# Where TensorE's filler work stands in a mixture-of-experts stage: products moved between routing, early and last expert pairs

## The reference, cut to what matters

```python
combine = jnp.einsum('tk,tke->te', gate, jax.nn.one_hot(e_idx, N_EXPERTS))
for e in range(N_EXPERTS):
    h = jax.nn.silu(xt @ w_gate[e]) * (xt @ w_up[e])
    y = y + combine[:, e:e + 1] * (h @ w_down[e])
...
h = _layernorm(DEEPNORM_ALPHA * h + ffn, ln_ffn_g[layer], ln_ffn_b[layer])
```

## Time and profile before

| | us |
|---|---|
| median of 3 timed runs | 1013.69 |
| lowest and highest | 1008.77, 1015.44 |
| time of the profiled execution | 1008.44 |
| span in its trace | 1006.5 |
| TensorE busy | 959.6 (95%) |
| mean DMA rate over the span | 276 GB/s read |

### The profile page before, as it was taken

One profiled execution on the slowest core, in us unless ns is written; L12 is line 12 of the kernel. 1 busy time (PEld: TensorE's weight loads), 2 busy tenths in 40 slices (PEclk: granted clock), 3 DMA queues, 4 the chain that ended last, 5 costly groups with the idle time before them and its releaser, 6 DMA issues.

```text
span 1006.5 us, 9999 instructions
## 1 busy us (share of the span) xinstructions
PE 959.6 (95%) x3984; PEld 512.8 (51%) x3984; DVE 298.7 (30%) x773; ACT 224.0 (22%) x466; POOL 15.2 (2%) x29
## 2 busy tenths in 40 slices
PE   8989999999999999989899999999998999999986
PEld 7644875554543335333385557888445334453321
DVE  4230162331521213120234433564316112121203
ACT  1120243221211112110211533431532111111101
POOL 2000000000000000000000000000000000000001
PEclk9999999999999999999999999999999999999999
DMA  8982424152789999999994423352555899999994
GB/s 274 335 316 85 160 92 167 43 209 83 302 327 388 422 421 421 421 419 422 398 386 143 168 84 124 127 210 82 210 209 218 323 406 421 421 421 421 418 419 165
DMA packets 65779, 278.84 MB, mean 277 GB/s; under 512 B 8852, under 2 KB 9216, under 8 KB 41920
## 3 DMA queue, kind: packets, MB, share of 16 engines
q1 hardware_dynamic: 63856, 271.60, 68.5%
q0 software_dynamic: 1872, 6.53, 1.9%
HBM read 277.04 MB, written 1.06 MB: 276 GB/s over the span
## 4 chain that ended last, share of the span: by engine, by line
PE 83%; DMA 11%; DVE 4%; ACT 1%; issue 1%; SPq 0%; DVEq 0%
PE bank L679 78%; DMA ring<-in_moe_w_up 10%; PE bank L1040 2%; DMA ring<-in_w_in_ab 1%; PE bank L1097 1%; PE bank L1045 1%; PE bank L1393 1%; PE bank L775 1%; ACT feat L1461 0%; PE bank L956 0%; DVE stat L2241 0%; ACT rstd L1461 0%; DVE feat L2223 0%; DVE hT L2248 0%; DVE h L2478 0%
## 5 line engine op out<-in xcount | busy, mean ns | idle before, releaser
L679 PE MATMUL bank<-ring,hT 128*64 128x512 f32 (+1 forms) x832 | 276.7, 597 | 8.9 <-DMA ring<-in_moe_w_up 4.1
L679 PE MATMUL bank<-ring,feat 128*64 128x512 f32 (+1 forms) x1152 | 226.3, 594 | 8.6 <-ACT feat L1461 4.1
L679 PEld LDWEIGHTS bank<-ring,hT 128*64 128x64 f32 (+1 forms) x832 | 109.8, 162 | 165.8 <-issue 157.8
L679 PE MATMUL bank<-hT,ring 128*128 128x256 f32 x768 | 168.4, 380 | 1.2 <-DMA ring<-in_w_in_ab 1.0
L679 PEld LDWEIGHTS bank<-hT,ring 128*128 128x128 f32 x768 | 145.8, 191 | 21.2 <-DMA ring<-in_w_in_ab 1.7
L679 PEld LDWEIGHTS bank<-ring,feat 128*64 128x64 f32 (+1 forms) x1152 | 74.3, 131 | 150.2 <-issue 140.8
L1461 ACT ACTIVATE feat<-bank 32x512 f32<-32x512 f32 (+3 forms) x128 | 61.1, 494 | 393.3 <-PE bank L679 251.3
L679 PE MATMUL bank<-ring,yT 128*128 128x512 f32 x256 | 112.8, 595 | 0.0
L2231 DVE COPY feat<-bank 32x512 f32<-32x512 f32 (+1 forms) x56 | 38.5, 687 | 150.4 <-PE bank L679 149.8
L679 PEld LDWEIGHTS bank<-ring,yT 128*128 128x128 f32 x256 | 47.8, 190 | 55.5 <-issue 54.6
L2223 DVE TENSOR_TENSOR feat<-feat,bank 128x512 f32<-128x512 f32 x16 | 11.0, 688 | 185.7 <-PE bank L679 185.7
(11 more groups left out here) (249 smaller groups left out, 549.9 us busy)
## 6 DMA issues: line engine op xcount, KB each, us to landing
ring<-in_moe_w_up SPq DMA_DIRECT2D x64, 1024.0 KB, 16.4
ring<-in_moe_w_gate SPq DMA_DIRECT2D x56, 1024.0 KB, 14.4
ring<-in_moe_w_down SPq DMA_DIRECT2D x56, 1024.0 KB, 13.0
ring<-in_w_in_ab SPq DMA_DIRECT2D x24, 1024.0 KB, 9.1
ring<-in_w_in_cd SPq DMA_DIRECT2D x24, 1024.0 KB, 12.7
ring<-in_w_out_ab SPq DMA_DIRECT2D x8, 1024.0 KB, 5.8
ring<-in_moe_w_down SPq DMA_DIRECT2D x16, 512.0 KB, 17.9
ring<-in_w_out_cd SPq DMA_DIRECT2D x8, 1024.0 KB, 6.1
```

Source lines behind the costliest of these rows:

```text
L679: return nc.tensor.matmul(o, l, r, start=start, stop=stop)
```

## The change

- `carry` for token block 0 moves from pairs 0 and 1 into `second_lists`, around `ranks(layer, 1)`: one matmul before it and one behind. `carry` for block 1 moves to the last pair, in front of `hid_turn` and in front of the last down product. The first spreading of block 1 then starts its banks (`start=True`).
- The gate product goes to bank 1 and the turned combine weights to bank 2; the pulls' banks are changed to suit.
- Chunks 0 and 1 of the gate products of pairs 1 and 2 (`AHEAD`) are done in the filler places of the pair before: chunk 0 in front of `hid_turn`, chunk 1 behind it.
- `weights_turn` of each quad goes from behind the odd pair's up product to the place in front of it.
- The gate product of pair 4 is interleaved with the last two gather products, as pair 0's already was.

```diff
+AHEAD = (1, 2)
-        first_pulls = ((0, 1, 0, 1), (2, 3, 0, 1))
+        first_pulls = ((0, 2, 0, 2), (1, 3, 0, 2))
+        second_pulls = ((0, 1, 2, 3), (1, 0, 2, 3))
...
+            def carry(layer, t, q):
+
+                if t == 0:
+                    claim(f"ffn{layer}", 4 + q)
+                nc.tensor.matmul(bank[4 + 2 * t + q][:, :], residual, h[:, t, q * 512:(q + 1) * 512],
+                                 start=t == 0, stop=False, skip_group_check=True)
...
                 pull(layer, 0, 0, 3)
+                carry(layer, 0, 0)
                 ranks(layer, 1)
+                carry(layer, 0, 1)
                 pull(layer, 0, 1, 0)
...
+                def gate_chunks(at, ks):
+
+                    i, pair = divmod(at, 2)
+                    if ks[0] == 0:
+                        claim(f"gate{layer}_{i}{pair}", 1)
+                        held_w[at] = [weights(at, e, KC) for e in range(2)]
+                    for k in ks:
+                        for e in range(2):
+                            last = mm(bank[1][e * 2 * SLOTS:(e + 1) * 2 * SLOTS, :],
+                                      slots_of(xg[i % 2][:, k, :], pair, e), held_w[at][e](k), k == 0, k == KC - 1)
+                        if k == KC // 2 - 1:
+                            last.then_inc(half_used, 1)
+                        if k == KC - 1:
+                            last.then_inc(ready[1], 1)
+
+                def first_gate(at):
+
+                    half = 2 * at // PAIRS
                     for j in range(4):
-                        pulled(0, j)
...
+                        pulled(half, j)
+                        gate_chunks(at, (2 * j, 2 * j + 1))
                         if j < 2:
-                            pull(layer, 0, 1, j + 2)
-                    last.then_inc(ready[2], 1)
+                            pull(layer, half, 1, j + 2)
...
                     for pair in range(2):
                         at = 2 * i + pair
...
+                        if at in (0, PAIRS // 2):
+                            first_gate(at)
                         else:
...
+                            gate_chunks(at, range(2 if at in AHEAD else 0, KC))
+                        if pair:
+                            claim(f"weigh{layer}_{i}", 2)
+                            pe.wait_ge(selw_ready, QUADS * layer + i + 1)
+                            weights_turn(2).then_inc(ready[2], 1)
                         claim(f"up{layer}_{i}{pair}", 3)
...
-                        if pair:
-                            claim(f"weigh{layer}_{i}", 1)
-                            pe.wait_ge(selw_ready, QUADS * layer + i + 1)
-                            weights_turn().then_inc(ready[1], 1)
-                        elif i:
+                        if i and not pair:
                             spread_out(i - 1, 0, 0)
                             spread_out(i - 1, 1, 0)
-                        if i == 0:
-                            carry(pair, 0)
+                        if at + 1 in AHEAD:
+                            gate_chunks(at + 1, (0,))
+                        if at == PAIRS - 1:
+                            carry(layer, 1, 0)
                         claim(f"hid{layer}_{i}{pair}", 0)
                         wait_stored(pe, f"up{layer}_{i}{pair}", 3)
                         hid_turn().then_inc(ready[0], 1)
...
-                        if i == 0:
-                            carry(pair, 1)
+                        if at + 1 in AHEAD:
+                            gate_chunks(at + 1, (1,))
+                        if at == PAIRS - 1:
+                            carry(layer, 1, 1)
                         wait_stored(pe, f"hid{layer}_{i}{pair}", 0)
```

More of the change, by code:

```diff
@@ L345, in moe_jobs @@
                         for j in range(4):
-                            job(f"pull{layer}_1{t}{j}", j)
+                            job(f"pull{layer}_1{t}{j}", second_pulls[t][j])
                 for pair in range(2):
-                    job(f"gate{layer}_{i}{pair}", 2)
+                    job(f"gate{layer}_{i}{pair}", 1)
+                    if pair:
+                        job(f"weigh{layer}_{i}", 2)
                     job(f"up{layer}_{i}{pair}", 3)
-                    if pair:
-                        job(f"weigh{layer}_{i}", 1)
                     job(f"hid{layer}_{i}{pair}", 0)
@@ L1092, in last_down @@
                                 last.then_inc(ready[2 + q], 1)
[L1094 to L1098, removed]
                 def pulled(half, j):
@@ L1122, in spread_out @@
                         wait_stored(pe, f"down{layer}_{i}{pair}", 2 + q)
-                    wait_stored(pe, f"weigh{layer}_{i}", 1)
-                    last = scatter(t, q)
+                    wait_stored(pe, f"weigh{layer}_{i}", 2)
+                    if i == 0 and t == 1:
+                        claim(f"ffn{layer}", 6 + q)
+                    last = scatter(t, q, start=i == 0 and t == 1)
                     if i == QUADS - 1:
@@ L1136, in experts @@
                     if i == 2:
[L1137 to L1142, removed]
+                        for t, j in ((0, 0), (0, 1), (0, 2), (0, 3), (1, 0), (1, 1)):
+                            pull(layer, 1, t, j)
                     for pair in range(2):
@@ L1145, in experts @@
                         rows = lambda k, e: slots_of(xg[i % 2][:, k, :], pair, e)
-                        if at == 0:
-                            first_gate(rows, [weights(0, e, KC) for e in range(2)])
-                        else:
-                            claim(f"gate{layer}_{i}{pair}", 2)
-                            dense_pair(2, rows, [weights(at, e, KC) for e in range(2)], KC, mid=half_used) \
-                                .then_inc(ready[2], 1)
+                        if at in (0, PAIRS // 2):
+                            first_gate(at)
+                        else:
+                            gate_chunks(at, range(2 if at in AHEAD else 0, KC))
+                        if pair:
+                            claim(f"weigh{layer}_{i}", 2)
+                            pe.wait_ge(selw_ready, QUADS * layer + i + 1)
+                            weights_turn(2).then_inc(ready[2], 1)
                         claim(f"up{layer}_{i}{pair}", 3)
@@ L1639, in moe @@
                     for pair in range(2):
-                        wait_ready(act, f"gate{layer}_{i}{pair}", 2)
-                        fn(sil, bank[2][:, :], ACT.Silu).then_inc(stored[2], 1)
+                        wait_ready(act, f"gate{layer}_{i}{pair}", 1)
+                        fn(sil, bank[1][:, :], ACT.Silu).then_inc(stored[1], 1)
                         wait_ready(act, f"hid{layer}_{i}{pair}", 0)
@@ L2220, in moe @@
                     for pair in range(2):
-                        wait_stored(dve, f"gate{layer}_{i}{pair}", 2)
+                        if pair:
+                            wait_ready(dve, f"weigh{layer}_{i}", 2)
+                            V.tensor_copy(selw_t.rearrange("p t n -> p (t n)"), bank[2][:, 0:TB * P]) \
+                                .then_inc(stored[2], 1)
+                        wait_stored(dve, f"gate{layer}_{i}{pair}", 1)
                         wait_ready(dve, f"up{layer}_{i}{pair}", 3)
```

29 lines of the change are left out of this document (8 added, 21 removed).

## The result

| | before | changed |
|---|---|---|
| median, 20 runs each | 1010.52 us | 1016.05 us |
| lowest to highest | 1006.86 to 1015.44 | 1013.36 to 1019.33 |
| profiled execution | 1008.44 | 1016.09 |
| its span | 1006.5 | 1014.2 |

The ratio is 1.005 with a 95% interval of 1.0038 to 1.0061: the change makes the kernel half a percent slower. The forecast was 1016.5, from a sum of +5.1 us; the ratio says +5.0 on 1010.5.

The account below looks back on a forecast made before the run. The weight stream was taken to set the expert stage. Terms 5.9 (wait) - 1.0 (routing) + 0.2 (tail) = +5.1 us, on the mean of 1011.6 giving 1016.7, stated as 1016.5; range 1007.0 to 1024.0.

Parts of the forecast that it names:

- Part 1: Routing: residual products fit TensorE's gaps and the clock drop goes; 1.0 us gained, in layer 0 alone.
- Part 2: Pair 0's gaps: chunks 0 and 1 of pair 1's gate replace residual products of the same length; 0 us.
- Part 3: Pair 1's gaps: TensorE waits for pair 2's gate weights, so the stream runs dry at pair 3; 5.9 us lost.
- Tail: Last pair: residual products now stand there, mostly covered; 0.1 us lost for each layer, 0.2 in all.
- the wait never bites: Rival, pair 1's gaps: weights in time or lateness absorbed, filled routing gaps save 1.0 us per layer; 1009.6, chance 0.13.
- the 7.7 to spare at pair 2: Pair 2's down weights: down product 1, 5.6 us late, does no harm, as 12.9 - 5.2 = 7.7 us are spare.
- TensorE catches up from pair 4 on: From pair 4: some 23 us a pair against the stream's 29.9, so lateness reaches no further; the stream's loss stays.
- That the clock stays up: Rival, behind pair 1's wait: no clock fall, stream dry for 0.6 and 0.9 us; +0.7, about 1012.3, chance 0.22.
- The long low clock: Rival: low clock through pair 1's down product costs 6.9 us in place of 1.5; +15.9, 1027.5, chance 0.1.
- The tail was covered: Rival, last pair: residual products not covered, 3.5 us on the tail in place of 0.2; 1020, chance 0.05.
- 1.8 to 2.0 to spare: Pair 3's down weights: TensorE may be late by 1.8 us in layer 1, 2.0 in layer 0, before the stream dries.
- 0.7 for a start from empty: Pair 3's down transfers: restarting the stream from an empty queue costs a further 0.7 us in each layer.

Follow-up runs that it names:

- the wait alone: Kernel before, with TensorE made to wait in pair 1, before the hidden turn, for the first halves of pair 2's gate weights; ratio 1.0072.
- pair 1 alone: Changed kernel, but only pair 1's gate is begun early and pair 2's is done in one piece; ratio 0.9974 against the kernel before.
- The run with the changed order: Changed kernel, with pair 4's gate weights issued ahead of pair 3's down weights; ratio 1.0055 against the kernel before.
- wait filled, 6: Changed kernel plus 6 further matmuls in pair 1 of each layer, before chunk 0 of pair 2's gate; ratio 1.0020 against the kernel before.
- wait filled, 12: Changed kernel plus 12 further matmuls in pair 1 of each layer, before chunk 0 of pair 2's gate; ratio 1.0077 against the kernel before.
- nothing early: Changed kernel with no gate product begun early, the other parts of the change kept; ratio 0.9992 against the kernel before.

## Why the prediction was right

**Right, by its steps.** Part 1: the first residual product leaves 0.22 us of the gap in front of the ranks, as stated, and the clock stays up. Part 2: hidden turn and down product of pair 0 are where they were, and down transfers of pair 1 are issued 21.3 us after the restart in both traces. Part 3: the wait is there, 5.67 and 6.85 us against 6.4 and 5.9; the clock falls behind it; the first transfer of pair 3's down weights lands in 5.0 and 4.9 us; the stream is dry in front of them. Tail: 0.1 us in each layer. The experiments show what the traces alone could not: the wait alone makes the kernel before slower, and the units' late release alone turns it into time.

**The total was closer than its terms, and that was luck.** The forecast sum was +5.1; the ratio says +5.0 and the ledger +6.0. But the term of the wait was too small and so was the gain, and the two errors cancel. The wait was put at 3.1 us in layer 0 and 2.8 in layer 1, 5.9 in all; the ledger has 2.8 and 4.0, 6.8 in all, and the comparison with pair 1 alone has 7.7 by the ratios and 8.0 by the traces (the intervals of the two ratios are 1.2 and 1.8 us wide to each side, so 5.9 is just inside). The rest of the change was put at 1.0 gained and 0.2 lost; by the ratio of pair 1 alone it gains 2.6 us, give or take 1.8. Part of what is missing is the routing, which was put at 1.0 us in layer 0 and nothing in layer 1. The two profiles agree with that, 1.05 and none, only because in the one of before the clock fell in layer 0 alone; over the four passages through the old routing it is 0.9 us in each layer, 1.8 in all. The gain that the rival "the wait never bites" counted on was thus there, and only its premise was false. The forecast of 1016.5 itself also stands on a base of 1011.4, against a measured median of 1010.52, so that the times differ by 5.5 us and not by 5.1.

**Sizes that were off.** In layer 1 the down product of pair 1 starts 45.33 us after the restart, against 37.45 before: 7.9 us late, not 5.6. Of the difference 0.9 lies in the steps from chunk 0 to the down product, which take 4.72 us where 2.3, their length before, and 1.5 for the clock were counted: the clock costs 2.1 us (4.72 against the 2.61 of the filled wait), and 0.3 is there without it. Another 1.3 is the landing of pair 2's gate, 40.6 us after the restart and not 39.3 (why it came later is open). With 7.9 us the 7.7 to spare at pair 2 were used up, hence the dip to 160 GB/s at 842 us that the prediction excluded. It changed the total little, because what the stream loses at pair 2 it has to spare at pair 3.

**A step that was weaker than put.** "TensorE catches up from pair 4 on" rested on 23 us a pair against 29.9 for the stream. The run with the changed order shows how little is made up: its lateness of 5.9 us at pair 3's turn (from the end of down product 2, 76.2 us after the restart, against 70.3) was 8.5 us at pair 4, behind a wait for the moved weights, and still 8.1 at pair 5, where the stream ran dry again. One pair, with the gather in it, made up 0.4 us. In the changed kernel itself the step did no harm: no window behind pair 3 falls below 380 GB/s.

**The rivals.** That the clock stays up is excluded for this stretch (0.50 in the windows of both layers; 328 to 330 us in layer 0). That the wait never bites is excluded by the trace. The long low clock did not come: the down product of pair 1 took its 6.95 us in layer 1 and 7.31 in layer 0. The tail was covered. The size of the whole rested on one view, the time from issue to landing. It gives the queue's depth at each transfer, and so the lateness at which an issue begins to cost; over eight pairs of layer and kernel the loss followed it (for the wait filled with 6, layer 1, by the last landing itself):

| kernel, layer | late | stream lost |
|---|---|---|
| wait filled, 6; layer 0 | 1.7 | 0.9 |
| before with wait; layer 0 | 3.4 | 2.3 |
| wait filled, 6; layer 1 | 3.4 | 2.1 |
| changed; layer 0 | 4.0 | 2.8 |
| changed; layer 1 | 5.3 | 4.0 |
| wait filled, 12; layer 0 | 6.2 | 5.1 |
| wait filled, 12; layer 1 | 6.7 | 5.2 |
| before with wait; layer 1 | 7.4 | 6.1 |

That is lateness less 0.8 to 1.4 us. The prediction's terms, 1.8 to 2.0 to spare and 0.7 for a start from empty, make 1.1 to 1.3. The Trainium skill, "DMA: Bandwidth & Descriptors", section "Anatomy of one DMA — SWDGE (gpsimd) path", gives a transfer some 2.0 us and its bytes over 436 GB/s, which is an estimate of 4.4 us for 1 MB. It states this fit for transfers issued from GpSimd, and these are issued by SyncE. The measured 4.9 and 5.0 us agree with the trace of before and not with that estimate, by which 0.6 us more would have been to spare in layer 0 and 0.8 in layer 1 (the prediction says 0.8 in each).

## What to carry to other kernels

Work that is pulled forward into a gap brings its waits with it. Before moving it, compare the landing time of what it reads with the time at which it will now stand in line, and ask what is queued behind it. In a kernel fed by a ring of buffers, the number that decides is how long before the queue is empty each buffer is released; the time from issue to landing, against that of a transfer into an empty queue, reads it off. And a hole in the stream is filled by releasing sooner what the next transfer waits for, not by issuing something else first.

## What the runs showed of the hardware that was not expected

TensorE's granted clock fell to 0.50 in the wait of 5.7 to 6.9 us and stayed there for some 5 us of work behind it, making steps last 4.7 us in both layers that took 2.61 where the wait was filled but for 0.6 and 1.8 us. Much shorter gaps close together bring it down as well, but not each time: two of 1.08 and 1.42 us did in three passages of four (one of two in the earlier trace rows, both in the run with the wait alone), two of 0.95 and 0.69 us in one layer and not in the other of the same execution (nothing early), and in the profile after it fell in the mixer (0.50 from 194 to 196 us) after a wait of 1.86 us that in the profile before had no such effect. So part of the spread of 8.6 us among 20 runs of the same kernel may be the clock; that was not tested.
